# MoE experts on one Trainium2 core: when the activations' second halves are transposed

## What is computed

```python
def moe_ffn(h, w_router, b_router, w_gu, b_gu, w_down, b_down):
    ...
    xs = hf[tok]                                    # rows sorted by expert
    gu = lax.ragged_dot(xs, w_gu, group_sizes) + b_gu[sorted_e]
    gate, up = jnp.split(gu, 2, axis=-1)
    gate = jnp.minimum(gate, SWIGLU_LIMIT)
    up = jnp.clip(up, -SWIGLU_LIMIT, SWIGLU_LIMIT)
    act = (up + 1.0) * (gate * jax.nn.sigmoid(SWIGLU_ALPHA * gate))
    out = lax.ragged_dot(act.astype(h.dtype), w_down, group_sizes) + b_down[sorted_e]
    out = out * weights.reshape(-1)[order][:, None]
    y = jnp.zeros((T, D), dtype=out.dtype).at[tok].add(out)
```

## Time and profile before

| | |
|---|---|
| median of three runs | 3969.74 us |
| the profiled execution, its span | 3969.4 us |
| TensorE matmul busy | 3789.1 us, 95% |
| VectorE busy | 2500.9 us, 63% |
| ScalarE busy | 1611.7 us, 41% |
| experts' stage, from the first expert matmul | 1211.1 us to the end |
| groups in it | 39 |

### The profile page before, as it was taken

The page is one execution under the profiler, slowest core; times in us unless marked ns, Lnnn a source line. Parts: engine busy times, 40 slices in busy tenths (PEclk is TensorE's granted clock), DMA queues, the critical chain, the costliest instruction groups (busy, mean ns, idle before and its releaser), DMA issues.

```text
span 3969.4 us, 66908 instructions
## 1 busy us (share of the span) xinstructions
PE 3789.1 (95%) x17917; PEld 3112.4 (78%) x17918; DVE 2500.9 (63%) x3917; ACT 1611.7 (41%) x2355; POOL 672.5 (17%) x712
## 2 busy tenths in 40 slices
PE   8999999898998999999999999999999999999995
PEld 5888788787876778878877877878888878888774
DVE  5363343696776786576577678587656565756764
ACT  3222321573223464354355454354334344433443
POOL 0110110111221211112112212132111102210301
PEclk9999999899998999999999999999999999999998
DMA  6442441664345797587588788597577567756755
GB/s 250 139 149 85 154 142 67 231 228 148 138 149 180 225 341 230 157 283 228 148 291 291 228 274 265 167 317 253 177 211 224 175 225 196 230 177 189 224 194 193
DMA packets 373240, 811.29 MB, mean 204 GB/s; under 512 B 31435, under 2 KB 31620, under 8 KB 368149
## 3 DMA queue, kind: packets, MB, share of 16 engines
q1 hardware_dynamic: 318210, 659.75, 48.3%
q0 software_dynamic: 49744, 133.33, 13.8%
q10 hardware_dynamic: 5220, 17.36, 1.1%
HBM read 704.36 MB, written 105.97 MB: 204 GB/s over the span
## 4 chain that ended last, share of the span: by engine, by line
PE 58%; DVE 8%; issue 5%; DMA 3%; DVEq 1%; ACT 1%; SPq 0%; ACTq 0%; POOLq 0%; POOL 0%
PE tok_bank_acc L119 15%; PE tok_bank_acc L121 15%; PE tok_bank_acc L120 15%; DVE weights_split L2176 2%; PE tok_bank_acc L2426 2%; PE tok_bank_acc L2427 2%; DMA weights_raw<-in_w_gu 1%; PE rou_bank_acc L119 1%; DVE weights_first L2176 1%; PE rou_bank_acc L121 1%; PE rou_bank_acc L120 1%; PE tok_bank_ta L2354 1%; PE tok_bank_tx L2346 1%; PE rou_bank_sm L1779 1%; DVE tok_act_row L2292 1%
## 5 line engine op out<-in xcount | busy, mean ns | idle before, releaser
L2076 ACT CAST weights_split<-weights_raw 128x1024 fp32r<-128x1024 f32 x468 | 475.9, 1054 | 401.3 <-PE tok_bank_acc L121 275.0
L2176 DVE TENSOR_TENSOR weights_split<-weights_raw,weights_split 128x1024 fp32r<-128x1024 f32 x468 | 545.5, 1218 | 27.1 <-ACT weights_first L2076 19.1
L2176 DVE TENSOR_TENSOR weights_first<-weights_raw,weights_first 128x1024 fp32r<-128x1024 f32 x464 | 538.2, 1217 | 8.3 <-ACT weights_first L2076 8.1
L2056 POOL DMA_INDIRECT y_rows<-tok_act_row,tok_token x110 | 216.1, 1965 | 1891.7 <-DVE tok_act_row L2292 1856.7
L2076 ACT CAST weights_first<-weights_raw 128x1024 fp32r<-128x1024 f32 x464 | 472.0, 1049 | 141.2 <-PE tok_bank_acc L121 95.2
L119 PE MATMUL tok_bank_acc<-weights_first,weights_split 128*128 128x512 f32 x1120 | 448.3, 400 | 9.5 <-DVE weights_first L2176 7.0
L119 PE MATMUL tok_bank_acc<-weights_split 128*128 128x512 f32 x1120 | 439.2, 392 | 2.1 <-DVE weights_split L2176 1.4
L121 PE MATMUL tok_bank_acc<-weights_first,weights_split 128*128 128x512 f32 x1120 | 438.0, 391 | 0.0
L120 PE MATMUL tok_bank_acc<-weights_first,weights_split 128*128 128x512 f32 x1120 | 437.0, 390 | 0.0
L121 PE MATMUL tok_bank_acc<-weights_split 128*128 128x512 f32 x1120 | 436.1, 389 | 0.0
L120 PE MATMUL tok_bank_acc<-weights_split 128*128 128x512 f32 x1120 | 435.9, 389 | 0.0
(11 more groups left out here) (393 smaller groups left out, 6986.3 us busy)
## 6 DMA issues: line engine op xcount, KB each, us to landing
weights_raw<-in_w_gu SPq DMA_DIRECT2D x624, 512.0 KB, 6.2
weights_raw<-in_w_down SPq DMA_DIRECT2D x312, 512.0 KB, 6.3
tok_bias<-in_b_gu SPq DMA_DIRECT2D x39, 1024.0 KB, 4.7
proj<-ent_stage SPq DMA_DIRECT2D x112, 256.0 KB, 2.0
early_w_raw<-in_w_in POOLq DMA_DIRECT2D x12, 2048.0 KB, 11.0
ent_w_ada<-in_w_ada POOLq DMA_DIRECT2D x64, 256.0 KB, 3.4
mix_late<-proj SPq DMA_DIRECT2D x48, 256.0 KB, 3.7
mod_w_ada<-in_w_ada SPq DMA_DIRECT2D x8, 1024.0 KB, 13.0
```

Source lines behind the costliest of these rows:

```text
L2056: pool.indirect_dma_start(out=keep["y"][c - NGU], out_offset=bass.IndirectOffsetOnAxis(ap=token[0:rows, t:t + 1], axis=0), in_=weighted_at ...
L2076: nc.scalar.copy(whi[c % 2][:, j * SK:(j + 1) * SK], raw[:, n % RAW]).then_inc(hi_done, 1)
L2176: nc.vector.tensor_tensor(wlo[c % 2][:, rows], raw[:, n % RAW], whi[c % 2][:, rows], ALU.subtract).then_inc(lo_done, 1)
```

## The change

On TensorE, `activations(G, 1, t)` for t > 0 no longer stands at s = 0 of tile t in chunk 4 but at s = 4 of the tile before it, behind that tile's own wait for `alo_done`. Which tile comes next depends on the group, so each place has an `If` for the next full tile and one for the half tile. In groups with one full tile, `next_row` now stands ahead of `activations(G, 1, 0)`. On VectorE, `activations_lo(1, t)` stands ahead of `weigh(4, t - 1)`, and `activations_lo(1, 0)` of groups with U > 2 stands inside chunk 3, behind `up_times_gate` of tile 1; other groups keep it where it was, under an `If`. ScalarE does the same with `activations_hi(1, 0)`, which in groups with U > 2 stands ahead of pieces 20 and 21. The instructions that compute are the same in number and size; the number of `If`s grows.

```diff
@@ scalar @@
-                for n in range(4 * PIECES + PIECES // 2, 5 * PIECES + PIECES // 2):
+                for n in range(4 * PIECES + PIECES // 2, 5 * PIECES):
                     weights_hi(g, n, G.chunks_before(n // PIECES - 1))
-                activations_hi(1, 0)
+                with act.If(G.U > 2):
+                    activations_hi(1, 0)
+                for n in range(5 * PIECES, 5 * PIECES + PIECES // 2):
+                    weights_hi(g, n, G.chunks_before(n // PIECES - 1))
+                with act.If(G.U < 3):
+                    activations_hi(1, 0)
@@ vector @@
-                activations_lo(1, 0)
+                        if c == NGU - 1 and t == 1:
+                            with dve.If(G.U > 2):
+                                activations_lo(1, 0)
+                with dve.If(G.U < 3):
+                    activations_lo(1, 0)
                 for n in range(5 * PIECES, 5 * PIECES + PIECES // 2):
                     weights_lo(g, n)
...
-                weigh(NGU, 0)
-                for t in range(1, SLOTS):
-                    with dve.If(G.has(t)):
+                for t in range(1, GT):
+                    with dve.If(G.T > t):
                         activations_lo(1, t)
+                        weigh(NGU, t - 1)
+                with dve.If(G.H > 0):
+                    activations_lo(1, HALF)
+                for t in range(GT):
+                    with dve.If(G.T == t + 1):
                         weigh(NGU, t)
+                with dve.If(G.H > 0):
+                    weigh(NGU, HALF)
@@ tensor @@
-                                if c == NGU and t > 0 and s == 0:
-                                    activations(G, 1, t)
                                 if c == NGU and t == 0:
                                     if s == 0:
                                         pe.wait_ge(alo_done, G.before * 2 + G.U + 1)
                                     if s == KD // 2:
+                                        next_row()
                                         with pe.If(G.T < 2):
                                             activations(G, 1, t)
-                                        next_row()
                                 if c == NGU and s == KD // 2:
                                     pe.wait_ge(alo_done, G.pair_tile(1, t))
+                                    if t + 1 < GT:
+                                        with pe.If(G.T > t + 1):
+                                            activations(G, 1, t + 1)
+                                    if t < GT:
+                                        with pe.If(G.half_at == t + 1):
+                                            activations(G, 1, HALF)
```

## The result

The changed kernel takes 3983.4 us (median; 3980.2 to 3985.9), against 3970.7 us for the kernel before on the same chip: a ratio of 1.003, 95% interval 1.0021 to 1.0039. That is 11.4 us over the forecast and 1.4 us over the upper end of its range. The profiled execution has a span of 3981.7 us, 12.3 more than before. Each experiment shifts them a little again; the tiles in a row tell what it is.

A forecast was written before the change was run, and what follows sets the result against it. PE, busy 95% of the span, was taken as the bound, with 42.4 us of waits touchable. Terms 5.5 + 0 + 1.2 - 2.9 - 0.8 - 0.8 = +2.2 us gave 3971.6 on the profiled span, 3972.0 as median; range 3957 to 3982.

The forecast's parts named there:

- 1+0 groups: Ten groups with one full tile and no half tile: chain not shortened, added control covered, 0 us in all.
- The second pause grows by as much: 0.: One full tile, no half: next_row (0.9 us) moves into PE's first pause, the second grows equally, net 0.
- PE arrives 1.1 us early for its load, so the 0.63 is covered: Next group's first weight load, timed by VectorE: 1.10 us of idle covers two new skipped Ifs, cost 0.
- 1+1 groups: Six groups with one full and one half tile: HALF's low part comes 0.2 us later, +1.2 us in all.
- 2+0 groups: Thirteen groups with two full tiles: weigh -0.66, VectorE's tests +0.45, PE's control +0.63, so +0.42 each, +5.5 us.
- 3+0: Seven groups with three full tiles: early low part and weigh remove the pause, -0.4 each, -2.9 us.
- 2+1 and 3+1: Three groups with two or three full tiles plus a half: shorter pause, -0.8 us for each kind.
- Slower: Rival: control isn't covered in 1+0 groups, 0.63 to 0.83 us each; 3980 to 3985 us, chance 0.23.
- Control is hidden: Rival: PE's sequencer runs the new Ifs early, 2+0 groups gain 0.6 us each; 3957 us, chance 0.17.
- All waits gone: Rival: the change removes all three PE waits for turned activations, -42 us, 3927 us, chance 0.03.
- The low-part wait: Sign in the profile after, 1+0 groups: PE's wait near 1.4 us idle instead of 0.44.
- The 0.4 us of issue ahead of the next group's first load: Sign in the profile after, behind 1+0 groups: about 0.4 us of issue instead of 1.10.

The follow-up runs named there:

- e1: Changed kernel with next_row moved back behind the activations' transposes in groups with one full tile: 3967.0 us, ratio 0.9987 to the kernel before.
- e2: Kernel before with only next_row moved ahead of the activations' transposes in groups with one full tile, no added Ifs: 3978.9 us, ratio 1.0016.
- e9: Kernel before with only VectorE's new order, low part of tile t ahead of weighing tile t - 1: 3952.7 us, ratio 0.9958.
- e5: e1 with PE's wait for the low part put behind the two Ifs of s = 4 in chunk 4: 3957.4 us, ratio 0.9963.
- e6: e1 with two more skipped Ifs behind the wait at s = 4 of tile 1 in chunk 4: 3974.2 us, ratio 1.0008.
- e3: Changed kernel with eight extra unused matmuls filling the pause ahead of the low-part wait in groups with one full tile: 3973.0 us, ratio 1.0001.
- e8: e1 with tile 0's second-half high and low parts made in the old places, without tests on U: 3966.4 us, ratio 0.999.
- e4: Changed kernel, rows still first, with the low-part wait put behind the two Ifs: 3962.2 us, ratio 0.9978.

## Why the prediction was wrong

The forecast was 3972.0 us in a range of 3957 to 3982; it came to 3983.4. Point by point:

- **1+0 groups: the step that failed.** "The second pause grows by as much: 0." The sizes were right: the pause grew, the chain did not move, and the skipped `If`s' 0.63 us were covered ahead of the next group's start (e1). What the step left out is that a pause isn't only idle time: it decides at which clock PE works afterwards. I counted the sum of both pauses and not how they are cut, and no term of my sum had the clock in it. It cost +11.7 us against 0. The step behind it, "PE arrives 1.1 us early for its load, so the 0.63 is covered", held for the 0.63 and not for the 1.7 us that the clock took on top.
- **1+1 groups: the same omission.** Four of six took +0.22 us, 0.2 forecast; the two with a half-clock stretch took +1.30 and +1.36. The composition held too: order +0.87 (e2), `weigh` -0.63 (e1, e9).
- **2+0 groups: right in mechanism, a little large in size.** +3.4 instead of +5.5 us, +0.26 a group instead of +0.42. `weigh` -0.65 (0.66), control on PE 0.62 (0.63), VectorE's tests 0.32 (0.45, bounds 0.28 to 0.6): the last is the term that was mis-sized. The control started only when the wait ended, as said, but for a plainer reason than the earlier trace rows: the wait was on the first `If`'s branch itself.
- **3+0: right**, -0.54 a group instead of -0.4; **2+1 and 3+1**, -2.0 instead of -1.6 us.
- **The rivals.** "Slower" has the right time, 3980 to 3985, and the wrong cause: control in 1+0 groups is covered. "Control is hidden" is refuted by e5 and e6. "All waits gone" didn't occur: the first two of the waits listed above alone are 33.3 us.
- **The signs to look for.** The low-part wait was to be near 1.4 us idle and is 2.06: 1.4 is what the order alone gives (e2), and I had not added the control to it, though I had priced it. Written down as 2.06, it would have stood above the transposes' waits of the earlier trace rows, 1.6 us on average, and been a reason to ask for the clock behind it. The 0.4 us of issue ahead of the next group's first load came true only behind the two groups without a fall. The sentence that the forecast is wrong if 1+0 groups take over 0.5 us longer came true in seven of ten.

**How sure.** That the clock's fall costs the time is shown: rows at 0.50 with 8 products instead of 16, no such stretch in e1 and e3, and e3 changes nothing but the empty time. That it hangs on the shape of the pauses is argued from five arrangements of the 1+0 group's first and second pause, with the number of these ten groups in which the clock fell. The lengths are from the start of PE's last instruction ahead of the pause to the start of the next, so the first ones come out some 0.2 us longer than in the expectations above: 1.9 and 0.7 us, none in the kernel before and one each in e5 and e9; 1.9 and 1.4, none in e1 and e8 and one in e6; 0.9 and 1.7, three in e2 and three in e4; 0.9 and 2.3, eight in the kernel after; the same, filled, none in e3. The single falls of e5, e6 and e9 (groups 37, 29 and 22) came right behind a first pause that was longer than usual, 2.4 to 2.5 us, as in e9 between the starts at 2649.53 and 2651.99. But length alone doesn't decide: first pauses of 2.35 to 2.5 us came nine times in all kernels, two of them in the kernel before (groups 13 and 29), and the clock fell behind three; and e2's 1+1 groups, with pauses of 1.7 and 1.8 us, had no fall, while pauses of 1.7 us in its 1+0 groups did. Why it is 8 and not 10, and 2 of 6 in the 1+1 groups with the same wait, stays open. What PE did ahead of a pause was not varied by itself. Not tried was e9 together with an early low part of tile 0 in the groups with three tiles; by the columns of e1 and e9 it could bring 1 us at most.

## What to carry to other kernels

When work that fills a pause is moved, look at how the empty pauses are cut, not only at the sum of idle time; if PE is otherwise full, ask for the granted clock behind each long one, since PE's busy time shows a slow stretch as work. Put a wait as late as the program allows: control behind a wait that is satisfied late is paid in full where nothing covers it, here some 0.3 us for each skipped `If`. And split a change by its engines: here VectorE's swap alone was worth 18 us, and the kernel with the other parts beside it is some 30 us slower than the swap alone.

## What was new about the hardware

- A pause of 2.3 us in a PE that is 95% busy, ahead of which stood eight transposes, a pause of 0.9 us and four more, was followed by 3.4 us or more at the 1.2 GHz level in eight of ten cases. Each such stretch took 1.7 us of PE's work; the eight groups became 1.4 us longer on average.
- The same 3.3 us of pause split as 1.9 and 1.4, with the eight transposes of `next_row` between, left the clock at 1.00 in all ten groups of e1, and eight matmuls whose results nobody uses made the changed kernel 10 us faster.
- Two skipped `If`s on PE's sequencer cost 0.62 us behind a pending wait (e1 against e5), and two more 0.55 (e6): each takes longer than the 0.23 us that a 128x512 product needs at full clock.
